# A router run between the tiles of the out-projection, and slot indices made on the chip instead of through a table in memory

## The reference, cut to what matters

```python
x = x + cross_attention(rms_norm(x, norm_x_g), rms_norm(mem, norm_mem_g), w_xq, w_xk, w_xv, w_xo)
x = x + hierarchical_moe(rms_norm(x, norm_ffn_g), ...)

# hierarchical_moe, 512 tokens of 1024 features, 4 groups x 8 experts, top 2
g_prob = softmax(xt @ w_rg + b_rg);  g_idx = argmax(g_prob);  g_w = g_prob[g_idx]
e_logits = (xt @ w_re + b_re).reshape(n_tok, 4, 8)[g_idx]
top_p, top_i = top_k(softmax(e_logits), 2)
comb = g_w * top_p / sum(top_p)
expert = g_idx * 8 + top_i
# every assignment (token, j) gets a place in its expert's list, in the order of tokens
yb = (silu(x_blk @ w1[e]) * (x_blk @ w3[e])) @ w2[e]      # for each expert's rows
out[token] += comb * yb
```

## Time and profile before

| | |
|---|---|
| median of 3 runs | 1952.68 us (1950.11 to 1956.24) |
| the profiled execution | 1949.07 us, its span 1947.8 us |
| TensorE busy (matmul) | 1639.2 us, 84% |
| VectorE, ScalarE, GpSimd busy | 752.8, 443.4, 272.9 us |
| mean granted TensorE clock | 0.928 of full |
| bytes moved | 324.32 MB, mean 167 GB/s |
| issues of expert weights | 96 of 2048 KB |

### The profile page before, as it was taken

How to read it: one execution, slowest core, us unless ns; L and a number is a source line. 1 busy time by engine, 2 the same in 40 slices (tenths; PEclk the granted TensorE clock), 3 DMA queues, 4 the chain that set the end, 5 groups by cost and what they waited for, 6 DMA issues and landing times.

```text
span 1947.8 us, 15235 instructions
## 1 busy us (share of the span) xinstructions
PE 1639.2 (84%) x5840; PEld 824.8 (42%) x5840; DVE 752.8 (39%) x1569; ACT 443.4 (23%) x899; POOL 272.9 (14%) x250
## 2 busy tenths in 40 slices
PE   6999957899999558888888787399879999997997
PEld 3344435754454323333333333254346545433653
DVE  2436166711333511110101111478955236895522
ACT  2001124200130100000000000214654331465431
POOL 0000000100000121111111110101850000185000
PEclk9999968999999779999989989698989999998999
DMA  8333104330612449999999996700200320020011
GB/s 299 121 139 130 43 1 151 130 130 12 226 57 97 164 172 412 409 408 406 404 400 407 396 399 287 278 1 22 92 1 1 147 97 1 22 92 0 1 65 43
DMA packets 71028, 324.32 MB, mean 167 GB/s; under 512 B 9322, under 2 KB 12690, under 8 KB 58528
## 3 DMA queue, kind: packets, MB, share of 16 engines
q1 hardware_dynamic: 62528, 306.96, 40.6%
q0 software_dynamic: 6016, 10.51, 1.7%
q10 hardware_dynamic: 2400, 5.73, 0.8%
HBM read 318.90 MB, written 12.67 MB: 170 GB/s over the span
## 4 chain that ended last, share of the span: by engine, by line
PE 61%; DMA 13%; DVE 11%; POOL 8%; ACT 3%; issue 2%; SPq 0%; POOLq 0%; DVEq 0%; ACTq 0%
PE bank L181 58%; DMA arena<-in_w 12%; POOL arena L2294 8%; DVE arena L2097 2%; DVE arena L2113 1%; PE bank L1776 1%; DVE arena L1454 1%; ACT arena L1014 1%; PE bank L499 1%; DVE arena L1052 1%; POOL arena L1492 1%; DVE arena L1462 0%; DVE arena L1164 0%; PE bank L1724 0%; PE bank L583 0%
## 5 line engine op out<-in xcount | busy, mean ns | idle before, releaser
L181 PE MATMUL bank<-arena 128*128 128x512 f32 (+9 forms) x4966 | 1523.5, 546 | 162.8 <-DVE arena L1462 42.0
L181 PEld LDWEIGHTS bank<-arena 128*128 128x128 f32 (+2 forms) x4966 | 713.0, 181 | 884.2 <-issue 772.1
L2294 POOL TENSOR_TENSOR arena<-arena 128x512 f32<-128x512 f32 x120 | 157.3, 1311 | 124.2 <-ACT arena L1978 107.0
L1492 POOL TENSOR_TENSOR arena<-arena 128x1 f32<-128x1 f32 (+2 forms) x44 | 38.3, 881 | 856.5 <-DVE arena L1043 519.5
L1454 DVE TENSOR_TENSOR arena<-arena,bank 64x512 f32<-64x512 f32 x32 | 22.1, 692 | 300.7 <-ACT arena L1014 300.7
L820 ACT COPY arena<-bank 128x512 f32<-128x512 f32 (+2 forms) x124 | 67.5, 551 | 305.5 <-PE bank L181 231.1
L1978 ACT ACTIVATE arena<-arena 128x512 f32<-128x512 f32 x120 | 85.6, 721 | 63.6 <-POOL arena L2294 63.6
L2097 DVE SCALAR_TENSOR_TENSOR arena<-arena 128x512 f32<-128x512 f32 x120 | 94.0, 783 | 3.3
L1513 POOL DMA_INDIRECT y_rows<-arena x32 | 32.4, 1011 | 436.4 <-PE bank L751 390.3
L1014 ACT ACTIVATE arena<-bank 64x512 f32<-64x512 f32 x32 | 18.9, 592 | 324.1 <-PE bank L181 324.1
L1451 DVE COPY arena<-bank 128x512 f32<-128x512 f32 x32 | 22.2, 693 | 151.0 <-PE bank L751 151.0
(11 more groups left out here) (258 smaller groups left out, 888.7 us busy)
## 6 DMA issues: line engine op xcount, KB each, us to landing
arena<-in_w SPq DMA_DIRECT2D x96, 2048.0 KB, 17.4
arena<-in_w_in SPq DMA_DIRECT2D x15, 2048.0 KB, 8.7
arena<-in_w_ada SPq DMA_DIRECT2D x12, 2048.0 KB, 9.0
arena<-in_w_out SPq DMA_DIRECT2D x6, 2048.0 KB, 9.1
arena<-in_w_xk SPq DMA_DIRECT2D x2, 2048.0 KB, 13.3
arena<-in_w_xv SPq DMA_DIRECT2D x2, 2048.0 KB, 8.7
arena<-in_w_xq SPq DMA_DIRECT2D x2, 2048.0 KB, 9.0
arena<-in_w_xo SPq DMA_DIRECT2D x2, 2048.0 KB, 8.6
```

What stands on the lines that cost most here:

```text
L181: i = pe.e.matmul(o, l, r, start=first and j == 0, stop=last and j == len(pairs) - 1)
L1492: pool.e.tensor_tensor(ss, ss, k.C("half").broadcast_to([128, ss.shape[1]]), ALU.pow).then_inc(*k.pool.step("root", *name))
L2294: pool.e.tensor_tensor(yc, yc, k.tmp[4 + n % 4], ALU.add).then_inc(*k.pool.step("sum", l, f, j))
```

## The change

The router's work is divided by tiles of 128 tokens, and the path to the indices no longer goes through memory.

- **Order.** TensorE runs tiles 0 and 1 of the out-projection, the transposes of tile 0 (`pe_router_turn`), tile 2, transposes of tile 1, tile 3, transposes of tile 2, logits of tiles 0 and 1, `pe_gate(1, 1)`, transposes of tile 3, logits of tiles 2 and 3. VectorE writes `XNf` of tile t where it did before, right after tile t+1's mean square, and then copies its half of the transposed tile.
- **Logits** now have the tokens' features as the standing operand and 40 router columns streaming (four columns of padding, so that max can read eight), so they come out with tokens on the partitions and need no transpose back.
- **Pick** runs in two halves of two tiles, with the transposed copy of tile 3 put into the first. The group's eight experts are selected by two products and one reduction. `asp` holds running sums of the one-hots over the tiles.
- **Ranks** come from matmuls (`rk`) of the triangle `before` and of ones. VectorE turns a rank into a one-hot over slots (`OHS`), and eight matmuls of `OHS` by `AHV` (the expert's one-hot times the assignment's number) give the table of slots in PSUM (`slot`). Three VectorE operations make `IDX` and `IDY`; then two buffers are cleared (`xg`), which GpSimd's first gather waits for.
- **The rest** (`dve_router_rest`: exponentials, weights, `DST`, the block list) moves behind the first expert's multiplication. The eight scatters to the table remain, behind GpSimd's first two gathers; only the extra blocks read the table.
- TensorE's out-projections take banks among the first seven.

```diff
+def pe_router_turn(k, pe, t):
+    for q in range(2):
+        b = k.banks.take(pe, k.dve if q else k.act, "tr", t, q, among=ROUTER_BANKS)
+        pe.wait_ge(*k.dve.done("xn", "f", t))
+        for f in range(4):
+            i = pe.e.transpose(b[:, f * 128:(f + 1) * 128],
+                               k.XNf[:, t, :].rearrange("p (q k) -> p k q", k=8)[:, 4 * q + f, :], k.ident)
...
 def pe_router(k, pe):
+    pe_out(k, pe, "w_xo", k.OT, (0, 1))
+    pe_router_turn(k, pe, 0)
+    pe_out(k, pe, "w_xo", k.OT, (2,))
+    pe_router_turn(k, pe, 1)
+    pe_out(k, pe, "w_xo", k.OT, (3,))
+    pe_router_turn(k, pe, 2)
+    pe_router_logits(k, pe, 0)
+    pe_gate(k, pe, 1, 1, ROUTER_BANKS)
+    pe_router_turn(k, pe, 3)
+    pe_router_logits(k, pe, 1)
+    pe_router_ranks(k, pe, 0)
+    pe_router_ranks(k, pe, 1)
+    pe_router_slots(k, pe, 0)
+    pe_router_slots(k, pe, 1)
...
+def dve_router_place(k, dve, u):
+    dve.e.tensor_tensor(k.PP[:, four, :].rearrange("p (t j) e -> p t j e", t=2), rank,
+                        k.AH[:, four, :].rearrange("p (t j) e -> p t j e", t=2), ALU.mult).then_inc(*V.step("rk", u))
+    dve.e.tensor_reduce(k.RK[:, four], k.PP[:, four, :], AX.X, ALU.add).then_inc(*V.step())
+    dve.e.tensor_tensor(k.OHS[:, four, :], C("iota").unsqueeze(1).broadcast_to([128, 4, 128]),
+                        k.RK[:, four].unsqueeze(2).broadcast_to([128, 4, 128]), ALU.is_equal).then_inc(*V.step("ohs", u))
...
     for e in range(NE + 1):
         if e < NE:
             dve_expert_up(k, dve, e)
+        if e == 0:
+            dve_router_rest(k, dve)
         if e:
             dve_expert_down(k, dve, e - 1)
...
+            if e == 0:
+                act.wait_ge(*V.done("ge"))
+                act.e.activation(k.GE, k.GE, ACT.Exp).then_inc(*A.step("ge"))
+                act.wait_ge(*V.done("ex"))
+                act.e.activation(k.ex, k.ex, ACT.Exp).then_inc(*A.step("ex"))
...
+    pool.wait_ge(*V.done("xg"))
+    pool.wait_ge(*k.h3_out.done("h3", 3))
+    pool_gather(k, pool, 0)
+    pool_gather(k, pool, 1)
     pool.wait_ge(*k.tab.done("clear"))
     pool.wait_ge(*V.done("dst"))
     for q in range(8):
         pool.e.indirect_dma_start(
             out=k.tab_d, out_offset=bass.IndirectOffsetOnAxis(ap=k.DSTU[:, q:q + 1], axis=0),
             in_=k.SIDU[:, q:q + 1], in_offset=None).then_inc(*k.scat.step(q))
-    pool.wait_ge(*V.done("idx"))
-    pool.wait_ge(*k.h3_out.done("h3", 3))
-    pool_gather(k, pool, 0)
-    pool_gather(k, pool, 1)
```

More of the change, by code:

```diff
@@ L253, in build @@
         base = ht_at + 4136
[L254 removed]
+        used = [NFREE - 320]
         def small(n):
@@ new lines, with pe_router_logits @@
+ROUTER_BANKS = range(7)
+def pe_router_turn(k, pe, t):
[5 more added lines that the diff above has]
+                               k.XNf[:, t, :].rearrange("p (q k) -> p k q", k=8)[:, 4 * q + f, :], k.ident)
+        i.then_inc(*k.pe.step("tr", t, q))
+def pe_router_logits(k, pe, u):
+    w = k.ring.at(("w_router",), 8, 40)
+    pe.wait_ge(*k.ring.landed(("w_router",)))
+    b = k.banks.take(pe, k.dve, "lg", u, among=ROUTER_BANKS)
+    for t in (2 * u, 2 * u + 1):
+        pe.wait_ge(*k.act.done("tr", t, 0))
+        pe.wait_ge(*k.dve.done("tr", t, 1))
+        lo = 40 * (t % 2)
+        i = product(pe, b[:, lo:lo + 40], [(k.HT[:, c, t * 128:(t + 1) * 128], w[:, c, :]) for c in range(8)])
+    i.then_inc(*k.pe.step("lg", u))
@@ new lines, in pe_router_ranks, with pe_router_slots @@
+def pe_router_ranks(k, pe, u):
+    b = k.banks.take(pe, k.dve, "rk", u, among=ROUTER_BANKS)
+    for t in (2 * u, 2 * u + 1):
+        if t:
+            pe.wait_ge(*k.dve.done("asp", u))
+        else:
+            pe.wait_ge(*k.dve.done("as", u))
+        pairs = [(k.C("ones"), k.ASP[:, t, :])] if t else []
+        lo = 32 * (t % 2)
+        i = product(pe, b[:, lo:lo + 32], pairs + [(k.C("before"), k.AS[:, t, :])])
+    i.then_inc(*k.pe.step("rk", u))
+def pe_router_slots(k, pe, u):
+    b = k.banks.at("slot") if u else k.banks.take(pe, k.dve, "slot", among=(7,))
+    pe.wait_ge(*k.dve.done("ohs", u))
+    pairs = [(k.OHS[:, q, :], k.AHV[:, q, :]) for q in range(4 * u, 4 * u + 4)]
+    i = product(pe, b[:, 0:32], pairs, u == 0, u == 1)
+    if u:
+        i.then_inc(*k.pe.step("slot"))
```

304 lines of the change are left out of this document (152 added, 152 removed).

## The result

Eight runs of each kernel: before 1953.45 us (1948.35 to 1957.46), changed 1963.03 us (1959.78 to 1965.74). The ratio is 1.0050, 95% interval 1.0034 to 1.0066. The change costs about 9.6 us, where the forecast had +1.8. The profiled execution of the changed kernel took 1965.74 us, its span 1964.4, the mean granted clock 0.924 (before: 0.928).

A forecast was written before the change was run, and what follows sets the result against it. The prediction took the experts' stream of weights as the bound. A gain of 8.4 us and a loss of 11.9 less 1.7 nearly cancel, leaving +1.8 on the median 1952.68: 1954.4 us, range 1947 to 1964.

The forecast's parts named there:

- rival (d): TensorE stays at half clock from tile 2's transposes to up 0: +9.4 us, 1963.8 us; chance 0.20.
- Out-projection: Two stops of 6.6 us each (wait, transposes, half clock) move its last addition from 642.84 to 656.5.
- rival (b): The clock stays at full in the stops, in tiles, logits, ranks and slots: 1947.5 us; chance 0.14.
- Transposes of tile 2 and logits: Router: transposes end at 661.4, first logits take 5.7 us, half clock until 3.45 us in; second logits end at 673.4.
- Pick, ranks, slots: Router: pick halves, then ranks at half clock and slots to 685.3; index operations and clears end at 688.0.
- Up 0: First expert's up product: transposes at 691.8, 7.09 us at full clock, Silu at 701.0; 8.4 us gained so far.
- The rest: Moved work holds VectorE 9.2 us ahead of expert 1's copy; up 1 at half clock, 9.74 us, ends at 722.2.
- The stream: Weight loads: queue empty until 722.2, first bytes at 723.2 against 721.4, so +1.8 us, then as before.
- the scatters cost nothing: The eight scatters, moved behind the first gathers, from about 703.5 to 713.8, were set to nothing.
- the sum: Whole program: the stream's +1.8 us added to the median 1952.68 gives 1954.4 us; chance 0.50.
- Rival (c): The moved rest costs nothing, since w1 and w3 of expert 2 keep the stream whole: 1944.3 us; chance 0.12.
- (e): Transposes do not count for the clock: 0.75 us more after each of three groups, 1956.7 us; chance 0.04.

The follow-up runs named there:

- rest ahead of Silu 0: Changed kernel with the rest of the routing between the copy of expert 0's tokens and the product with its Silu: 1960.54 us, ratio 1.0021.
- the old router with the new counters: Kernel before, with the second block's two PSUM bank counters set to the changed kernel's values, 2 and 6: 1961.57 us, ratio 1.0025.
- counters 4 and 0: Changed kernel with the second block's bank counters (eight banks, first seven) set back to those of the kernel before: 1959.52 us, ratio 1.0018.
- counters 0 and 4: Changed kernel with the second block's bank counters set to 0 for the eight banks and 4 for the first seven: 1967.27 us, ratio 1.0063.
- early scaling: Changed kernel with VectorE scaling tile t ahead of the addition of tile t+1: 1948.23 us, ratio 0.9946.
- all mends without scatters: Changed kernel with early scaling, rest behind expert 0's token copy, clears, products and gather 2 moved, counters 4 and 0, no scatters: 1927.91 us, ratio 0.9857.
- the first try at the mends: Changed kernel with early scaling, rest behind expert 0's token copy, clears ahead of the second pick, products moved, counters 4 and 0: 1943.84 us, ratio 0.9935.
- the rest at expert 4: Changed kernel with the rest of the routing, its count product and the eight scatters moved from expert 0 to expert 4: 1980.13 us, ratio 1.0120.

## Why the prediction was right in its parts and off in its size

The measured 1963.03 lies inside the range of 1947 to 1964, near its upper end, and on the slower side, to which 0.20 had been given. The change was forecast at +1.8 us and cost 9.6, 7.8 more. That the time still falls inside the range is luck: the upper end was set by rival (d), and most of what was missed comes from a block that the forecast did not look at. Against its steps:

1. **Out-projection.** Said: last addition at 656.5, two stops of 3.4 us of wait, half clock behind each. Measured 656.04; stops 3.36 and 3.34. The first half waited 0.87 us for its bank, said 0.4 and at most 0.5. The grant fell in the first only (0.57 over 618 to 626, tile 2 2.0 us longer) and stayed at 1.00 in the second. Right, with one of the two clock terms missing. One reading was off: the first row, 0.53 over 646 to 647, puts the fall at 646.1 and not near 646.5, so 3.2 us behind the last product and not 3.7, which favours rival (b) less.
2. **Transposes of tile 2 and logits.** Said 5.7 us for the first pair. Measured 8.74 (with the gate's two records): the grant was 0.50 for all of 660 to 670, not for 3.45 us. Second logits and gate 5.30, said 4.9. They end at 675.9, 2.5 later than said.
3. **Pick, ranks, slots.** Said 688.0 for the end of the clears, measured 689.0 (the gather starts at 689.82). Ranks and slots ran at half clock, as said, but the reason given (TensorE idle from 674) does not hold: the grant fell at 673.7, while TensorE was still at the second logits. The working also has 681.9 where its terms give 680.2 + 2.0 = 682.2, which changes nothing.
4. **Up 0.** Said: transposes 691.8, Silu 701.0, 8.4 us gained. Measured 692.93, 702.00, 7.4 us.
5. **The rest.** Said 9.2 us and 9.74 for up 1, Silu 1 at 722.2. Measured 9.2, 9.44 and 722.78. The run with the rest ahead of Silu 0 got 6 of the 11.9 us back.
6. **The stream.** Said +1.8 at its end, measured +2.6 by the averages. Right, as far as they can tell. That the scatters cost nothing was right too, but only in this kernel, with a hole to lie in. The other term set to nothing, gather 2, held here as well; it cost 1.08 us once the hole was half closed.

**The step that failed is the sum.** It set the end of the program equal to the end of the stream: "an expert stage that starts s us earlier ends s us earlier", and the sum adds +1.8 to the whole. The banks were looked at only where the change names them (+0.4 at the first half of the out-projection). That the same counters give out the second block's banks was in the code and in the listed change, and it was worth 5 to 6 us: 4.9 by the old router with the new counters, 6 by the new router with the old ones, 5.7 by the profiles' averages.

Rival (d), a clock at half from tile 2's transposes to up 0, gave 1963.8, which is nearly the time that came out, for another reason. Its mechanism came true in part: behind the third stop the grant was at 0.50 from 660.1 to 670.3 and from 673.7 to 690.8, with TensorE at narrow matmuls when it fell at 673.7. But the second logits began at full clock (0.93 over 670 to 674, 0.79 over the whole 5.3 us) and up 0 ran at 7.09 us, and all of it made Silu 0 1.0 us later than forecast, not 9.4. Rival (b) came true in the second stop alone. Rival (c) is refuted by the hole after 712. On (e): the Trainium skill, "TensorE: Matmul & The Clock Gate", section "Part 4: PE-mode transpose", has transposes not count as busy. Full clock returned 5.8 us after work resumed behind the first stop (transposes, then wide matmuls) and 10.9 us behind the third (transposes, then narrow ones), against 4.95 in the earlier trace rows with transposes alone. By the page's rule it would be an estimated 6.45 (the 4.95 and 1.5 us of transposes ahead of them). The first is nearer to that than to the forecast's 4.95; the third fits neither. No run was made to settle it.

The Trainium skill, "Perfetto Trace Analysis", section "Matmuls", says that independent matmul groups should rotate through different PSUM banks so that copies overlap the next group. All kernels of the table do. The change, its run with counters 4 and 0 and its run with 0 and 4 differ in nothing but where the rotation stands, and the last two are 0.45% (9 us) apart in time: rotating is not enough, it also matters who held the bank before.

One difference stays open. In five kernels (the change, early scaling, rest ahead of Silu 0, counters 0 and 4, all mends without scatters) TensorE starts the second block's first transposes 4.4 to 5.2 us after VectorE has their operand, with nothing that it waits for; the chain of waits of the change:

```profile
1250.84 0.76 DVE arena L2369
1251.60 4.75 issue
1256.35 3.69 PE bank L1817 x16
```

In the others this gap is 0.2 to 1.8 us. Ahead of it TensorE walks past the 15 skipped blocks for extra tokens, and a slower walk in some layouts of the program would fit, but no run was made for it. It may carry some of the time: from the last Silu to the first exponential these five take 234.9 to 236.4 us, the other profiles with 4 and 0 230.9 to 235.1 and the other two with 2 and 6 233.2 and 232.9. The change has the gap, and the same kernel with counters 4 and 0 does not, so some 2 us of what came back there may be due to this gap and not to the banks. The run with the old router is free of it, since neither it nor before has the gap; its 4.9 us are the cleaner figure.

## What to carry to other kernels

A resource that is dealt out by a running counter (banks, ring slots, buffers) carries a change to every later user, so list the takes of both programs to their end and compare whom each group waits for, above all the groups that stand first behind a slow producer. Where an engine in fixed order waits for a norm or a copy, look first whether the writer has long had its input and does other work ahead of it: one reordering on VectorE gave 20 us here, twice what the change had lost. Work moved out of one gap needs a gap that is longer than itself and a release of what it holds (a bank, a queue) that nobody needs sooner; four experts later it cost more than where it came from, and in the first try at the mends it kept a bank that up 0 needed. What lies hidden in a hole, as the scatters did, has to be priced anew when the hole is closed.

## What was not expected of the hardware

- Two stops of the same length had different clocks. Around the stop of 3.36 us the grant was at 0.50 from 619.1 to 625.9; around that of 3.34 us it never fell. This is no chance of one execution: in all six profiles with these stops the grant falls at the first, 22.9 us behind VectorE's first addition, stays up at the second and falls again 0.7 us behind the end of the third. With the early scaling, which has neither stop, both stretches are at 1.00.
- The grant stayed at 0.50 for the whole window from 660 to 670 above, though TensorE worked through all of it (logits of 40 columns, then the gate and transposes). With the early scaling it fell at 652.0, though TensorE had been at work since 591.2 without a stop, the last 3.1 us at such logits: the grant can fall without idleness.
- Eight scatters of 128 words each (4 KB in all) took some 2.6 MB of room from the stream of weights, as shown above.
- The stretches of the expert stage scatter more than those around it. From Silu 1 to the last Silu pass 482.0 to 489.2 us in the kernels with scatters (without the run with the rest at expert 4), 484.4 and 482.4 in two profiles of the same kernel; from the last exponential to the end 79.5 to 79.6 in each.
